# A two-layer hybrid trunk on one core: retention's last turn in another bank, rounds and score steps in other places, three constant products

## What is computed

```python
for l in range(DEPTH):
    h = rmsnorm(x, norm_mix[l])
    proj = h @ w_in[l]
    (u, dq, dk, dv, iq, ik, iw, rq, rk, rv, rg) = jnp.split(proj, split_pts, axis=-1)
    y_a = s5_mixer(u, ...)
    y_b = dsa_attention(dq.reshape(...), dk, dv, iq.reshape(...), ik, iw, rel_bias)
    y_c = retention(rq, rk, rv, rg, ret_gn[l])
    x = x + concatenate([y_a, y_b, y_c]) @ w_out[l]
    h = rmsnorm(x, norm_ffn[l])
    gate, up = jnp.split(h @ w_ffn_in[l], 2, axis=-1)
    x = x + (silu(gate) * up) @ w_ffn_out[l]
return rmsnorm(x, norm_final)
```

## Time and profile before

| | us |
|---|---|
| median of 3 runs (2666.86, 2672.77, 2673.14) | 2672.77 |
| profiled execution | 2670.3 |
| its span | 2668.5 |
| PE busy in the span | 2551.4 (96%) |
| DVE busy | 1553.0 (58%) |
| POOL busy | 1308.9 (49%) |
| ACT busy | 1020.3 (38%) |
| mean granted TensorE clock | 0.987 |

### The profile page before, as it was taken

One profiled execution on the slowest core, in us unless ns is written; L12 is line 12 of the kernel. 1 busy time (PEld: TensorE's weight loads), 2 busy tenths in 40 slices (PEclk: granted clock), 3 DMA queues, 4 the chain that ended last, 5 costly groups with the idle time before them and its releaser, 6 DMA issues.

```text
span 2668.5 us, 34623 instructions
## 1 busy us (share of the span) xinstructions
PE 2551.4 (96%) x13515; PEld 2007.8 (75%) x13515; DVE 1553.0 (58%) x2691; ACT 1020.3 (38%) x1478; POOL 1308.9 (49%) x818
## 2 busy tenths in 40 slices
PE   8998979999999999999999999999999999999998
PEld 6766757677777777778777787777777777888887
DVE  3769767799997226833331385677999922211111
ACT  5232354244435433324344422442534453322222
POOL 3332344455545564536555532544555447665654
PEclk9988999999999999999999999999999999999998
DMA  5341112132222153323322242222222215233332
GB/s 165 85 132 41 49 53 90 52 91 72 78 71 64 58 189 95 87 64 91 91 77 82 80 138 56 79 60 76 77 77 60 79 44 201 79 103 103 108 110 82
DMA packets 385666, 232.91 MB, mean 87 GB/s; under 512 B 29593, under 2 KB 371553, under 8 KB 383073
## 3 DMA queue, kind: packets, MB, share of 16 engines
q1 hardware_dynamic: 385136, 229.62, 29.0%
q10 hardware_dynamic: 368, 1.08, 0.1%
HBM read 213.88 MB, written 14.69 MB: 86 GB/s over the span
## 4 chain that ended last, share of the span: by engine, by line
PE 68%; DVE 25%; ACT 3%; issue 3%; POOL 1%; DMA 1%; DVEq 0%; ACTq 0%; SPq 0%
PE psum L1759 65%; DVE scores L1361 7%; DVE top L1359 7%; PE psum L2079 1%; DVE psum L1395 1%; DVE xs L1179 1%; DVE scores L1347 1%; DVE tmp L1319 1%; ACT w_hi L835 0%; ACT scratch L1036 0%; POOL w_lo L724 0%; DVE tmp L1308 0%; DVE scratch L1428 0%; PE psum L2176 0%; ACT xs L1054 0%
## 5 line engine op out<-in xcount | busy, mean ns | idle before, releaser
L724 POOL TENSOR_TENSOR w_lo<-w_raw,w_hi 128x1024 fp32r<-128x1024 f32 (+2 forms) x408 | 900.8, 2208 | 1197.9 <-ACT w_hi L835 1197.8
L1759 PE MATMUL psum<-h_hi,w_hi 128*128 128x512 f32 x1984 | 796.4, 401 | 15.2 <-ACT h_hi L859 7.4
L835 ACT ACTIVATE w_hi<-w_raw 128x1024 fp32r<-128x1024 f32 (+2 forms) x408 | 397.7, 975 | 1047.9 <-PE psum L1759 989.4
L1759 PE MATMUL psum<-h_lo,w_hi 128*128 128x512 f32 x1984 | 763.2, 391 | 0.9 <-POOL h_lo L732 0.9
L1759 PE MATMUL psum<-h_hi,w_lo 128*128 128x512 f32 x1984 | 514.4, 390 | 0.0
L1759 PEld LDWEIGHTS psum<-h_hi,w_hi 128*128 128x128 f32 x1984 | 374.9, 189 | 128.3 <-issue 36.1
L1759 PEld LDWEIGHTS psum<-h_lo,w_hi 128*128 128x128 f32 x1984 | 373.9, 189 | 78.3 <-issue 1.9
L1759 PEld LDWEIGHTS psum<-h_hi,w_lo 128*128 128x128 f32 x1984 | 373.3, 188 | 76.6
L1359 DVE MAX8 top<-scores 128x8 f32<-128x512 f32 (+5 forms) x352 | 324.3, 921 | 7.8
L1361 DVE MATCH_REPLACE8 scores<-top,scores 128x512 f32<-128x512 f32 (+5 forms) x352 | 319.0, 906 | 0.0
L1179 DVE TENSOR_TENSOR xs<-xs,psum 128x512 f32<-128x512 f32 x160 | 109.6, 686 | 315.0 <-PE psum L1759 304.5
(11 more groups left out here) (310 smaller groups left out, 2913.5 us busy)
## 6 DMA issues: line engine op xcount, KB each, us to landing
w_raw<-in_w_ffn_in_dram SPq DMA_DIRECT2D x176, 512.0 KB, 3.8
w_raw<-in_w_ffn_out_dram SPq DMA_DIRECT2D x96, 384.0 KB, 3.1
w_raw<-in_w_in_dram SPq DMA_DIRECT2D x68, 512.0 KB, 3.8
w_raw<-in_w_out_dram SPq DMA_DIRECT2D x32, 512.0 KB, 3.6
x_half<-xs SPq DMA_DIRECT2D x8, 1024.0 KB, 6.5
xs<-x_half SPq DMA_DIRECT2D x8, 1024.0 KB, 6.9
w_raw<-in_w_ffn_out_dram SPq DMA_DIRECT2D x32, 256.0 KB, 2.7
out_dram<-mixed SPq DMA_DIRECT2D x8, 512.0 KB, 4.5
```

The costliest lines, as they stand in the source:

```text
L724: eng.tensor_tensor(w_lo(u, n), w_raw[:, u % 3, 0:n], w_hi[:, u % 2, 0:n].bitcast(F32), ALU.subtract).then_inc(sems["weights_ready"], 1)
L835: act(w_hi[:, u % 2, 0:n], w_raw[:, u % 3, 0:n], ACTF.Copy).then_inc(sems["hi_ready"], 1)
L1759: return eng.matmul(out_, lhsT, rhs, start=start, stop=stop, skip_group_check=True)
```

## The change

It has six edits.

1. proj(0,1): the rounds of block 3 that `place` puts ahead of units i4 to i10 stand elsewhere: none at i4 (two before), two at i5 behind retention step 12, one at i6 behind step 13, then 2, 0, 2, 2 for i7 to i10 (before 1, 0, 2, 1). In all as many.
2. Retention's last turn (step 13 on PE, its copy in step 14 on ACT) lies in bank D, not C, in all four (l, h).
3. `late(l)`: in mixout(l,0) i4 carries two rounds of block 4, i5 score step 3, i6 two rounds; before, i4 to i6 carried score steps 3, 4 and 5 with two rounds each behind 4 and 5 and none behind 3. Score steps 4 and 5 go to ffn(l,0) ahead of steps 6 to 8, and two more rounds with them.
4. `weave` over ffn(l, h) ends at its length less 9 units, not less 11, in `mix_and_ffn` (the halves (0,0), (1,0) and (1,1)).
5. ACT waits for `mat_ready` in ffn at tile f == 2, not at f == 0.
6. `idle_products`: at retention step 4 of (0,0), ahead of its waits, PE makes three products of the table of ones and the decay table (128x128 by 128x512, float32) in bank half C1; nobody reads them.

```diff
@@ plan
-                 ret[11:12] + s5[:1] + three[:2], s5[1:2] + ret[12:13] + three[2:4], ret[13:] + s5[2:3] + three[4:5],
-                 s5[3:4] + prep[4:5] + three[5:6], s5[4:6] + prep[5:], s5[6:7] + three[6:8], s5[7:9] + three[8:9],
+                 ret[11:12] + s5[:1], s5[1:2] + ret[12:13] + three[:2], ret[13:] + s5[2:3] + three[2:3],
+                 s5[3:4] + prep[4:5] + three[3:5], s5[4:6] + prep[5:], s5[6:7] + three[5:7], s5[7:9] + three[7:9],
@@ late
-        lead += [sc[n:n + 1] + rounds(4, 2 * n - 6, 2 * n - 4) for n in range(3, 6)]
-
-        side = blend(sc[6:] + ret[2:9], rounds(4, 6, 27)) + blend(ret[9:], rounds(4, 27))
+        lead += [rounds(4, 0, 2), sc[3:4], rounds(4, 2, 4)]
+
+        side = blend(sc[4:] + ret[2:9], rounds(4, 4, 27)) + blend(ret[9:], rounds(4, 27))
@@ mix_and_ffn
-        got += ffn[:1] + scales() + weave(ffn[1:], side, 0, len(ffn) - 11)
+        got += ffn[:1] + scales() + weave(ffn[1:], side, 0, len(ffn) - 9)
@@ ACT, ffn
-                            if f == 0:
+                            if f == 2:
                                 eng.wait_ge(sems["mat_ready"], st.now("mat_ready"))
@@ ACT, retention step 14
-                    act(ret_o, bank("C").rearrange("p (a c) -> p a c", a=2), ACTF.Copy).then_inc(sems["ret_ready"], 1)
+                    act(ret_o, bank("D").rearrange("p (a c) -> p a c", a=2), ACTF.Copy).then_inc(sems["ret_ready"], 1)
@@ PE
+            def idle_products(g, n):
+
+                take(g)
+                for _ in range(n):
+                    mm(bank(g), ones, table("decay"), True, True)
@@ PE, retention steps 4 to 7
+                    if (l, h, c) == (0, 0, 0):
+                        idle_products("C1", 3)
                     if c == 0:
                         eng.wait_ge(sems["qs_ready"], st.add("qs_ready"))
@@ PE, retention step 13
-                    take("C")
+                    take("D")
                     for a in range(2):
                         for t in range(TT):
-                            ins = eng.transpose(bank("C", a * 512 + t * P, a * 512 + (t + 1) * P),
+                            ins = eng.transpose(bank("D", a * 512 + t * P, a * 512 + (t + 1) * P),
                                                 r_in[:, t, 0, a * P:(a + 1) * P], ident)
                     ins.then_inc(sems["ro_turned"], 1)
-                    leave("C", "ret_ready")
+                    leave("D", "ret_ready")
```

## The result

The changed kernel takes 2675.48 us (median of 16 runs, 2670.54 to 2682.39), the kernel before 2670.97 (16 runs, 2664.44 to 2675.63). The ratio is 1.0018 with a 95% interval of 1.001 to 1.0025: 4.8 us slower, and clear of zero though smaller than the 8 us that the forecast treated as no change. The forecast was 2658. The profiled execution of the changed kernel took 2673.61, span 2671.8, against 2670.3 and 2668.5.

A forecast was written before the change was run, and what follows sets the result against it. PE, busy 2551.4 of 2668.5 us, was taken as the bound. Part A's -2.4 and the two layers' -12.0 took 2670.3 to 2655.9; with 2.5 for the median, 2658 us, range 2648 to 2675.

The forecast's parts named there:

- Products: Retention step 4 of (0,0): three constant products fill PE's gap of 2.65 us and keep full clock, -4.4 us.
- R3: Rival, chance 0.10: products don't hold the clock and gaps only move to the next step; -2 us, 2671.
- Rounds and bank D: proj(0,1): turn's 5.25 us wait nearly goes, but VectorE's meetings with POOL splits cost; +2 us, -1.1 to +6.5.
- Part A: First outputs and proj(0,1) together: -4.4 + 2.0 = -2.4 us, bounds -8.9 and +10.1.
- Ahead of the dense zone: Late region, each layer: gaps of 1.41, 1.07 and those ahead of score steps shrink by 1.4, 0.5, 0.4; together -2.3 us.
- the tail: Last attention steps, each layer: 8.5 us of gaps and low clock become four gaps, 4.8; saving 3.7, bounds 0 and 7.
- The dense zone: 563 to 846 us: same 42 units carry the same rounds and attention steps; 0, bounds -4 to +4.
- R2: Slower rival, chance 0.11: VectorE backlog in ffn, 8.5 us per layer moved into 455 to 563; +7 us, 2680.

The follow-up runs named there:

- no_products: The changed kernel without the three constant products: 1.0031 of the kernel before, 3.5 us above the changed kernel.
- bank_rounds: The kernel before with only the moved rounds of block 3 and the last turn in bank D: 1.0012, +3.2 us.
- early_only: The changed kernel with late(l), window and f as before, so only products, rounds of block 3 and bank D: 0.9999 of the kernel before, -0.3 us.
- late_w11: The changed kernel with the window's end at less 11 again: 1.0129 of the kernel before, 30 us slower than the changed kernel.
- late_only: The kernel before with the changed late(l), window less 9 and wait at f == 2, nothing in proj(0,1): 1.0027, +7.2 us.

## Why the prediction was wrong

- **Products: right, to size.** -4.4 was forecast; the marks give -3.9 alone (-5.5 in the changed kernel, 120.26 against 125.72 in no_products), the timed runs 2.9 and 3.5, and the trace -4.2 at the very next conversion (162.31 against 167.18, less 0.64 that the changed trace was early by the 21st). The clock behind the filled gap is 1.00. R3's half of this is out.
- **Rounds and bank D: right sum, wrong reason for one half.** +2 was forecast, within -1.1 to +6.5; -2.75 + 3.9 = +1.1 in the changed kernel's trace, +2.7 by no_products (125.72), and +3.2 (timed) or +3.4 (trace) in bank_rounds. The step "With bank D the turn waits only for retention's own output, so of 5.25 some 0.3 is left" gave the bank a credit that belongs to the rounds: with bank D alone 5.68 was left, as its own output is what stands just ahead of the eviction, with the rounds alone 1.56, and with both none in the changed kernel's trace and 1.94 in early_only's. The mechanism named for the loss, meetings with POOL's splits, is in the rows (2.84, 2.84, 4.79, 2.71) and its 2.5 us lie within the 0 to 3.2 allowed. "VectorE is the bound here", on the other hand, was too strong: it was full, but its work moved with PE's, or the products' gain would have been lost.
- **Part A in all: not contradicted**, -2.4 forecast, -2.75 and -1.0 in two traces, timed -0.3 (-2.9 to +2.7).
- **Ahead of the dense zone: this is the step that failed.** "Of the 1.07 at 562.42 half, -0.5, as steps 10 and 11 now share a unit and the turn has a unit of its own". It went from 1.07 to 6.40: 5.3 + 0.5 = 5.8 off in each layer, before the clock. I read the step's place in the list, not what else its new neighbours put in the three queues: an up unit has an eviction on VectorE, an activation on ScalarE and a product on POOL, and the down units that the norm left have only an addition. The wait for a square root had been priced in proj(0,1), at 0.35, and was not looked for here. The other gaps there (1.48, 1.51, 1.50 and 1.41, in sum 5.9) became 1.14, 1.11, 1.50 and 0.94 (4.7): -1.2, where -1.8 was forecast, with a new wait at the first ffn unit and low clock there that I had not expected. (The 1.50 stands ahead of a retention turn, L2106, not of a score step.)
- **Low clock in the late regions: a term that the sum hasn't got.** It has the tail's -1.6 and nothing for new waits ahead of it. By the nine traces the changed late half costs 0.6 (layer 0) and 3.6 us (layer 1) more by work at 0.50 than the one before, the tail's gain already in it; in the changed kernel's own trace layer 1 pays 5.9.
- **The dense zone: right, but by the window.** 0 with -4 to +4 was taken because the same 42 units carry the same steps. In the changed kernel that held, PE's gaps inside it being 8.7 before and 8.0 after. But it held only through the wider window, and I never separated the two: late_w11 has the zone without it, with 12.1 of gaps, and its late regions are 20.9 and 16.0 us longer.
- **The tail: right**, -3.7 forecast, -3.6 by the gaps and the clock.
- **R2, the slower rival, had the right cause and the wrong place and price.** The move of VectorE's work into ffn is what cost the time, 10.7 us at equal window. It was to show as VectorE over 95% busy in 455 to 563; there it is 82.99 of 108 us (77%), less than the 84.41 before. The idle time was there, but not where the norm needed it. I gave this case 0.11, since I weighed the idle of a whole stretch. By the forecast's own rival list, 2675.5 lies between R3 and R2, just above the range's end of 2675.

What stays open: why layer 1 pays more for the clock than layer 0 with the same waits. In the changed kernel its low stretches lie at the gaps at 1737, 1870 and 2288, in the kernel before only at the one at 2184; in late_only and no_products they lie at the same three places, so it isn't an accident of one execution. Edit 5 by itself, and a window at less 5, weren't run.

## What to carry to other kernels

Price a move by the neighbours that it gets, queue by queue: the row to look for is the same step elsewhere in the trace, beside the same kind of unit. When a change shifts work and widens the room for it in one go, price the two apart, for the sum says nothing of either: here 10.7 us of loss and 5.6 of gain stood in two edits of one diff, and the second, carried further, was worth 12 us more (9 with the changed late(l)). A new wait has a price beside its length, the low clock around it, and a sum over waits needs a term for it. And an engine that is full isn't the bound if its work is released by the engine that waits for it.

## What the runs showed of the hardware

- Three float32 products of constants, 2.84 us of work whose result nobody reads, kept the granted clock at 1.00 where a wait of 2.65 was followed by 0.50 for 10 us. The stretch at 0.50 is in all six traces without the products and in none of the fourteen with them.
- The same wait isn't always followed by the same clock. The gap of 1.13 near 2288 in the changed kernel has a low stretch behind it and the same 1.13 at 2285.66 in the kernel before has none.
- A low clock ahead of another wait can be free. Seven kernels have the same program in proj(0,1) (with the square root in step 12): four give 120.3 us for it and three 122.0. The four have a low stretch at the 3.59 wait (207.96 in the changed kernel), no wait at the turn, and then one of 6.41; in the three the clock stays up there, the turn waits 1.9, and 2.3 and 4.3 follow. Why the four come out faster isn't shown. So a single trace's stage is uncertain by 1.7 us here, and by more in the late regions: over the six traces with the late half of before they spread by 2.7 and 4.0 us.
- A scan on VectorE is held up by a POOL split like a product of two operands: eight scans took 4.79 us beside the split at 241.01 (one of them 2.55, the others 0.4) and 2.63 without one.
- A small operation's table load (1.28 us, ahead of the 0.22 us square root) is part of its price on ScalarE, and an order that lets the load run while VectorE still computes hides it (in the kernel before it was loaded at 551.03, 3.0 us ahead of the root, and VectorE didn't wait).
